# Layer 0 of a hybrid encoder in two halves, its projections first and in seven half products a pair

## The reference, cut to what matters

```python
def pool_mixer(h, w_in, w_group, scale, w_out):     # h = rms_norm(x, pool_norm)
    proj = h @ w_in                                  # (1024, 1024) @ (1024, 4096)
    u, gate = proj[..., :2048], proj[..., 2048:]
    ug = u.reshape(B, S, 4, 512)                     # four groups, windows 2, 4, 8, 16
    pooled = stack([centred_window_mean(ug[:, :, g], w) for g, w in enumerate((2, 4, 8, 16))])
    diff = pooled - ug
    mixed = einsum('bsgc,gcd->bsgd', diff, w_group).reshape(B, S, 2048) * scale
    return (mixed * silu(gate)) @ w_out              # (1024, 2048) @ (2048, 1024)
```

## Time and profile before

| | |
|---|---|
| median of 3 runs | 1842.08 us (1841.94 to 1842.33) |
| the profiled execution | 1842.04 us |
| its span | 1840.1 us |
| TensorE busy | 1823.5 us, 99% |
| VectorE busy | 872.9 us, 47% |
| ScalarE busy | 546.4 us, 30% |
| GpSimd busy | 154.0 us, 8% |

### The profile page before, as it was taken

One profiled execution on the slowest core, in us unless ns is written; L12 is line 12 of the kernel. 1 busy time (PEld: TensorE's weight loads), 2 busy tenths in 40 slices (PEclk: granted clock), 3 DMA queues, 4 the chain that ended last, 5 costly groups with the idle time before them and its releaser, 6 DMA issues.

```text
span 1840.1 us, 22883 instructions
## 1 busy us (share of the span) xinstructions
PE 1823.5 (99%) x8976; PEld 1538.2 (84%) x8976; DVE 872.9 (47%) x1728; ACT 546.4 (30%) x976; POOL 154.0 (8%) x236
## 2 busy tenths in 40 slices
PE   7999999999999999999999999999999999999999
PEld 7888888888888788888889888888888888888887
DVE  5544434633564543454156425523585415532575
ACT  4311211121221422343235424322421323422420
POOL 1000000000000410111011201110100101110100
PEclk9999999999999999999999999999999999999999
DMA  5211111111111421111111111111245111111234
GB/s 173 59 51 41 58 46 46 46 58 35 57 46 58 136 66 58 35 61 55 46 41 53 47 46 47 58 46 37 68 168 176 47 46 41 52 47 46 69 116 159
DMA packets 90506, 121.54 MB, mean 66 GB/s; under 512 B 14369, under 2 KB 52129, under 8 KB 90401
## 3 DMA queue, kind: packets, MB, share of 16 engines
q1 hardware_dynamic: 74304, 85.90, 15.3%
q10 hardware_dynamic: 16096, 34.19, 5.2%
HBM read 99.04 MB, written 21.04 MB: 65 GB/s over the span
## 4 chain that ended last, share of the span: by engine, by line
PE 97%; DVE 2%; DMA 0%; ACT 0%; issue 0%; POOL 0%; ACTq 0%; DVEq 0%; POOLq 0%
PE pair L617 28%; PE pair L619 28%; PE pair L618 28%; PE pair L841 4%; PE pair L819 4%; PE pair L809 2%; PE pair L828 2%; PE pair L630 0%; PE pair L797 0%; DMA xs<-in_x_dram 0%; DVE xs L895 0%; DVE hTl L911 0%; DVE bufS L919 0%; DVE bufU L919 0%; ACT squares L1257 0%
## 5 line engine op out<-in xcount | busy, mean ns | idle before, releaser
L617 PE MATMUL pair<-w,hTh 128*128 128x512 f32 x1280 | 515.3, 403 | 0.8 <-DVE xs L895 0.8
L619 PE MATMUL pair<-w,hTl 128*128 128x512 f32 x1280 | 500.7, 391 | 0.0
L618 PE MATMUL pair<-w,hTh 128*128 128x512 f32 x1280 | 499.4, 390 | 0.0
L619 PEld LDWEIGHTS pair<-w,hTl 128*128 128x128 f32 x1280 | 244.2, 191 | 50.7
L617 PEld LDWEIGHTS pair<-w,hTh 128*128 128x128 f32 x1280 | 244.6, 191 | 45.2 <-DVE xs L895 1.0
L618 PEld LDWEIGHTS pair<-w,hTh 128*128 128x128 f32 x1280 | 245.0, 191 | 43.9
L888 DVE TENSOR_TENSOR w<-raw,w 128x1024 fp32r<-128x1024 f32 x140 | 169.3, 1222 | 218.9 <-ACT w L1230 218.0
L617 PE MATMUL pair<-hTh,w 128*128 128x512 f32 (+1 forms) x560 | 209.0, 373 | 0.9 <-DVE hTl L911 0.9
L618 PE MATMUL pair<-hTl,w 128*128 128x512 f32 (+1 forms) x560 | 208.3, 372 | 0.0
L619 PE MATMUL pair<-hTh,w 128*128 128x512 f32 (+1 forms) x560 | 208.2, 372 | 0.0
L1230 ACT ACTIVATE w<-raw 128x1024 fp32r<-128x1024 f32 x144 | 149.8, 1052 | 141.7 <-PE pair L619 141.3
(11 more groups left out here) (119 smaller groups left out, 2200.1 us busy)
## 6 DMA issues: line engine op xcount, KB each, us to landing
raw<-in_att_w_in_dram SPq DMA_DIRECT2D x80, 512.0 KB, 3.7
raw<-in_pool_w_in_dram SPq DMA_DIRECT2D x32, 512.0 KB, 4.4
raw<-in_pool_w_out_dram SPq DMA_DIRECT2D x16, 512.0 KB, 3.4
u_spill<-ub ACTq DMA_DIRECT2D x32, 256.0 KB, 2.2
ub<-u_spill SPq DMA_DIRECT2D x32, 256.0 KB, 3.8
xb<-x_spill ACTq DMA_DIRECT2D x16, 512.0 KB, 4.4
xs<-in_x_dram ACTq DMA_DIRECT2D x8, 512.0 KB, 5.6
raw<-in_pool_w_group_dram SPq DMA_DIRECT2D x8, 512.0 KB, 3.5
```

What stands on the lines that cost most here:

```text
L617: nc.tensor.matmul(out, lh, rh, start=first, stop=False)
L618: nc.tensor.matmul(out, lh, rl, start=False, stop=False)
L619: return nc.tensor.matmul(out, ll, rh, start=False, stop=last)
```

## The change

Layer 0 gets two halves. In the first, all projections are made: six plain blocks (U(0,0..3), G(0,0), G(0,1)), then 13 couples of two feature blocks, U and G in turn. A couple is a product of a 256 x 1024 by a 1024 x 1024 matrix, taken as 2 x 2 blocks, in seven products (`couple`), each of 4 `kd` x 3 = 12 matmuls of 128x512. For that GpSimd adds high and low parts of the activations up again (`put_together`), VectorE makes four sums of their quarters (`turned_sums`) and ScalarE and VectorE split them once; for each couple GpSimd makes four sums of the weights' quarters (`weight_sums`), and ScalarE and VectorE split seven pieces of 512 (`split_product`) into a ring of ten half slots. The results stand in three banks X, Y and W; the three parts that two outputs share are copied out (`keep`) and added (`add_quarter`). The banks of odd and even couples differ. Raw buffers are freed in twos, after the low part of a couple's last piece.

The windows work in memory (`ubuf`), and diff and silu(gate) of every block are stored to DRAM: `diff_spill` and `gate_spill`, 16 blocks of 512 KB each. x is not kept: it is loaded again. In the second half come the M and O jobs of all groups, and diff and gate are loaded back into eight stage buffers in the room of the activations, over SyncE's queue. The calls of `split_hi`, `split_lo`, `diff_high`, `diff_low`, `z_first`, `z_high` and `z_low` there have the same operations and shapes as before, in a new order. The diff, cut to its core:

```diff
+    PLAIN = [("U", 0, 0), ("U", 0, 1), ("U", 0, 2), ("U", 0, 3), ("G", 0, 0), ("G", 0, 1)]
+    u_couples = [("U", g, h) for g in range(1, NG) for h in range(GB // 2)]
+    g_couples = [("G", 0, 1)] + [("G", g, h) for g in range(1, NG) for h in range(GB // 2)]
+    COUPLES = [k for both in zip(u_couples, g_couples) for k in both] + g_couples[len(u_couples):]
+    NCOUPLE, NPROD = len(COUPLES), 7
...
+        jobs = [("M", 0, 0)]
         for g in range(NG):
-            jobs.append(("U", g, 0))
-            if g:
-                jobs += [("O", g - 1, 1, tb) for tb in range(TB)]
-            jobs += [("U", g, c) for c in range(1, GB)]
-            jobs += [("G", g, 0), ("M", g, 0), ("G", g, 1), ("M", g, 1), ("G", g, 2)]
-            jobs += [("O", g, 0, tb) for tb in range(TB)]
-            jobs += [("M", g, 2), ("G", g, 3), ("M", g, 3)]
-        jobs += [("O", NG - 1, 1, tb) for tb in range(TB)]
-        pair_of = {j: n % 4 for n, j in enumerate(jobs)}
+            jobs += [("M", g, 1), ("M", g, 2)] + [("O", g, 0, tb) for tb in range(TB)] + [("M", g, 3)]
+            if g < NG - 1:
+                jobs.append(("M", g + 1, 0))
+            jobs += [("O", g, 1, tb) for tb in range(TB)]
...
+        def raw_released(u):
+            if NPLAIN <= u < LATER:
+                return w_lo, product((u - NPLAIN) // 2, NPROD - 1) + 1
+            return lo_ready(u)
...
-                    inverse_roots(layer, *range(TB))
+                    inverse_roots(layer, *range(5))
+                    for tb in range(TB):
+                        put_together(tb)
+                        if tb < 3:
+                            inverse_roots(layer, 5 + tb)
...
+            def put_together(tb):
+                pool.wait_ge(hlo_done, tb + 1)
+                tokens_ = slice(P * tb, P * tb + P)
+                nc.gpsimd.tensor_tensor(whole[:, :, tokens_], rowsh[:, :, tokens_].bitcast(F32),
+                                        rowsl[:, :, tokens_].bitcast(F32), ALU.add).then_inc(whole_set, 1)
+            def weight_sums(n):
+                for i in range(2):
+                    u = NPLAIN + 2 * n + i
+                    pool.wait_ge(raw_in[u % RAW], 16 * (u // RAW + 1))
+                if n:
+                    pool.wait_ge(w_lo, product(n - 1, 5) + 1)
+                else:
+                    pool.wait_ge(g_done, 2)
+                a11, a12, a21, a22 = (raw[:, 0, 0:512], raw[:, 0, 512:1024], raw[:, 1, 0:512], raw[:, 1, 512:1024])
+                nc.gpsimd.tensor_tensor(sums[0], a21, a22, ALU.add).then_inc(s_sum, 1)
+                pool.wait_ge(s_sum, 4 * n + 1)
+                nc.gpsimd.tensor_tensor(sums[1], sums[0], a11, ALU.subtract).then_inc(s_sum, 1)
+                nc.gpsimd.tensor_tensor(sums[2], a11, a21, ALU.subtract).then_inc(s_sum, 1)
+                pool.wait_ge(s_sum, 4 * n + 2)
+                nc.gpsimd.tensor_tensor(sums[3], a12, sums[1], ALU.subtract).then_inc(s_sum, 1)
...
+            def couple(n):
+                X, Y, W = couple_banks(n)
+                moving = [(X, lambda kd: (rowsh[:, kd, left], rowsl[:, kd, left])),
+                          (W, lambda kd: (rowsh[:, HB + kd, left], rowsl[:, HB + kd, left])),
+                          (X, lambda kd: (tone[:, HB + kd, left], tone[:, HB + kd, right])),
+                          (Y, lambda kd: (tone[:, kd, left], tone[:, kd, right])),
+                          (X, lambda kd: (ttwo[:, kd, left], ttwo[:, kd, right])),
+                          (Y, lambda kd: (rowsh[:, HB + kd, right], rowsl[:, HB + kd, right])),
+                          (X, lambda kd: (ttwo[:, HB + kd, left], ttwo[:, HB + kd, right]))]
+                for i, (out, rhs) in enumerate(moving):
+                    if i == 0:
...
+                    elif i == 2:
+                        pe.wait_ge(kept, 3 * n + 1)
+                        if n == 0:
+                            pe.wait_ge(t_lo, 4)
+                    elif i == 3:
+                        if n >= 2:
+                            pe.wait_ge(c_added, 3 * (n - 2) + 3)
+                    elif i == 4:
+                        pe.wait_ge(kept, 3 * n + 2)
+                    elif i == 5:
+                        pe.wait_ge(kept, 3 * n + 3)
+                    else:
+                        pe.wait_ge(c_added, 3 * n + 2)
+                    pe.wait_ge(w_lo, product(n, i) + 1)
+                    wh, wl = (product_view(n, i, lo).rearrange("p (k c) -> p k c", k=HB) for lo in (False, True))
+                    for kd in range(HB):
+                        rh, rl = rhs(kd)
+                        last = three(out, wh[:, kd, :], wl[:, kd, :], rh, rl, kd == 0 and i in (0, 1, 3),
+                                     kd == HB - 1, i not in (0, 1, 3))
+                    last.then_inc(prod_done, 1)
...
+            def turned_sums():
+                upper, lower = slice(0, KD // 2), slice(KD // 2, KD)
+                left, right = slice(0, T // 2), slice(T // 2, T)
+                b11, b12, b21, b22 = (whole[:, upper, left], whole[:, upper, right], whole[:, lower, left],
+                                      whole[:, lower, right])
+                dve.wait_ge(whole_set, TB)
+                nc.vector.tensor_tensor(b22, b22, b12, ALU.subtract).then_inc(t_sum, 1)
+                nc.vector.tensor_tensor(b12, b12, b11, ALU.subtract).then_inc(t_sum, 1)
+                dve.wait_ge(t_sum, 2)
+                nc.vector.tensor_tensor(b11, b22, b11, ALU.add).then_inc(t_sum, 1)
+                dve.wait_ge(t_sum, 3)
+                nc.vector.tensor_tensor(b21, b21, b11, ALU.subtract).then_inc(t_sum, 1)
+            def turned_low(i):
...
                 link(nc.vector.tensor_tensor(ends, ends, edge[:, g, :, :], ALU.mult))
-                mid = src[:, PAD:PAD + T]
-                nc.vector.scalar_tensor_tensor(out=mid, in0=mid, scalar=1.0 / w, in1=pair[pair_of[("U", g, c)]][:, :],
-                                               op0=ALU.mult, op1=ALU.subtract).then_inc(d_ready, 1)
-                split_lo(after(("U", g, c)))
+                nc.vector.scalar_tensor_tensor(out=u[:, PAD:PAD + T], in0=src[:, PAD:PAD + T], scalar=1.0 / w,
+                                               in1=u[:, PAD:PAD + T], op0=ALU.mult, op1=ALU.subtract).then_inc(d_ready, 1)
...
+            def add_quarter(n, i):
+                X, Y, W = couple_banks(n)
+                src, h, p, q, right = ((W, 0, 2, 0, 0), (X, 2, 5, 1, 1), (Y, 1, 6, 0, 1))[i]
+                kind, g, hh = COUPLES[n]
+                dve.wait_ge(prod_done, NPROD * n + p)
+                dve.wait_ge(kept, 3 * n + h + 1)
+                if i < 2:
+                    dve.wait_ge((d_out if kind == "U" else g_out)[q], 16 * (GB // 2 * g + hh))
+                dst = ubuf[:, q, PAD:PAD + T] if kind == "U" else gbuf[q][:, :]
+                nc.vector.tensor_tensor(dst[:, 512 * right:512 * right + 512], src, held[h], ALU.add).then_inc(c_added, 1)
+            def couple_windows(n):
+                kind, g, hh = COUPLES[n]
+                if kind == "U":
+                    dve.wait_ge(c_added, 3 * n + 3)
+                    window(g, 2 * hh)
+                    dve.wait_ge(c21_done, n + 1)
+                    window(g, 2 * hh + 1)
...
+            add_quarter(0, 0)
+            split_product(1, 0)
+            split_product(1, 1)
+            add_quarter(0, 1)
+            split_product(1, 2)
+            add_quarter(0, 2)
+            for i in range(3, NPROD):
+                split_product(1, i)
+            couple_windows(0)
+            for i in range(3):
+                split_product(2, i)
+            for n in range(1, NCOUPLE):
+                if n < NCOUPLE - 1:
+                    split_product(n + 1, 3)
+                    add_quarter(n, 0)
+                    for i in range(4, NPROD):
+                        split_product(n + 1, i)
+                    add_quarter(n, 1)
+                    add_quarter(n, 2)
+                    couple_windows(n)
+                    if n < NCOUPLE - 2:
+                        for i in range(3):
+                            split_product(n + 2, i)
+                    else:
+                        split_lo(LATER)
...
+                if 2 <= i < 6:
+                    act.wait_ge(s_sum, 4 * n + (2, 1, 3, 4)[i - 2])
+                p = NPROD * n + i
+                if p >= GRANULES - 2:
+                    act.wait_ge(*((prod_done, p - GRANULES + 1) if p >= GRANULES else (g_done, 2)))
+                elif p < 6:
+                    act.wait_ge(u_done, p // 2 + 2)
...
+            def keep(n, i):
+                X, Y, W = couple_banks(n)
+                act.wait_ge(prod_done, NPROD * n + (1, 3, 4)[i])
+                if n:
+                    act.wait_ge(c_added, 3 * (n - 1) + (1, 3, 2)[i])
+                else:
+                    act.wait_ge(g_done, 2)
+                nc.scalar.activation(held[i], (X, X, Y)[i], ACT.Copy).then_inc(kept, 1)
...
+            keep(0, 0)
+            for i in range(3, NPROD):
```

(79 more changed lines are left out.)

484 lines of the change are left out of this document (342 added, 142 removed).

## The result

| | before | after |
|---|---|---|
| median of 20 executions | 1841.98 us (1841.29 to 1842.85) | 1845.8 us (1842.95 to 1847.29) |
| the profiled execution | 1842.04 us | 1844.97 us |
| its span | 1840.1 us | 1842.4 us |

The ratio is 1.002, with a 95% interval of 1.0014 to 1.0026: slower by about as little as can be told from no change. The forecast was 1836.5 us and faster. The saving of 35.3 us came in full, and 37.6 us instead of 29.8 were given back: 35.3 and the 2.3 by which the profiled span is longer (by the medians, 3.8 us apart, it is 39.1).

What follows compares the result with a forecast made beforehand. TensorE's matmul count was taken as the bound while helpers stay hidden. Of 35.3 us saved, 29.8 would be returned, so 5.5 gained: 1842.0 to 1836.5 us, range 1814 to 1856.

Steps and rivals of the forecast that it cites:

- The saving of 35.3 us: Layer 0's thirteen couples: 84 matmuls instead of 96 each, 156 fewer at 0.226 us, saving 35.3 us.
- the pitch of 0.226 us: TensorE in layer 0: one 128x512 matmul starts 0.226 us after another, taken as the cost of each.
- rival 1: GpSimd's sums hardly hold VectorE up and the start stalls are short: 1812 to 1819 us, chance 0.2.
- rival 2: VectorE's chain of window steps keeps GpSimd's sums out until it ends: 1859 us, chance 0.13.
- start, until couple 0: Before the couples: GpSimd's put_together delays inverse roots and VectorE's scaling and low half, making TensorE wait: 3 us.
- couple 0, product 2: Plain projections cover the turned sums and four w=2 windows; if that fails, product 2 waits up to 3 us.
- couple 1's keep: ScalarE's copy stands behind splits of couple 2 that need late weights and sums: 6.1 us, paid once.
- behind windows of w=8 and 16: VectorE's addition for product 6 comes late after two windows slowed by GpSimd's sums: four stalls, 14.6 us.
- keeps behind late splits: Late splits delay loads and ScalarE's next keep; with gate stores, 0.8 after each of four G couples: 3.2 us.
- hand-overs and slower clock: Added for hand-overs and a slower clock behind the longer stalls: 2 us, a guess between 0 and 5.
- M and O jobs: Rest of layer 0 covered, except the last O weights' split after z at the end: 0.9 us.
- Rival 3: As forecast, but loads beside stores land 1 to 2 us later and the clock falls: 1842 to 1850 us, chance 0.2.

Runs made afterwards that it cites:

- no_sums: The changed kernel without GpSimd's four sums of each couple's weights, raw pieces split instead, so values differ from the reference; 1815.37 us, ratio 0.9857.
- keep_first: The changed kernel with ScalarE's copy of a couple's first product ahead of the next couple's three splits; 1837.97 us, ratio 0.9977.
- odd_window_later: The changed kernel with each U couple's second window moved on VectorE behind the next couple's splits and additions; 1827.8 us, ratio 0.9921.
- first_two: The changed kernel with keep_first and odd_window_later together, the start as changed; 1822.61 us, ratio 0.9893.
- held_4: The kernel before the change with TensorE held at six places of layer 0 by four small GpSimd operations each; 1891.94 us.
- held_2: The kernel before the change with TensorE held at six places of layer 0 by two small GpSimd operations each; 1871.58 us.
- held_9: The kernel before the change with TensorE held at six places of layer 0 by nine small GpSimd operations each; 1925.77 us.
- start_and_end: The changed kernel with keep_first, odd_window_later and roots_first, plus four further reorderings at the start, couple 1 and couple 12; 1816.05 us, ratio 0.9859.
- roots_first: The changed kernel with GpSimd making all eight inverse roots before adding up the activations; 1846.38 us, ratio 1.0023.
- all_three: The changed kernel with keep_first, odd_window_later and roots_first together; 1823.39 us, ratio 0.9895.
- held_1: The kernel before the change with TensorE held at six places of layer 0 by one small GpSimd operation each; 1851.6 us.

## Why the prediction was wrong

What was right: the pitch of 0.226 us and the 35.3 us; that VectorE's window steps and GpSimd's sums exclude each other and alternate, so that neither rival 1 nor rival 2 came; the places of the waits. The terms of what is given back, beside what they measured:

| term | forecast, us | measured, us |
|---|---|---|
| start, until couple 0 | 3 | 5.6 |
| couple 0, product 2 | 0 | 0.8 |
| couple 1's keep | 6.1 | 9.1 |
| behind windows of w=8 and 16 | 14.6 | 11.8 |
| keeps behind late splits | 3.2 | 2.5 |
| hand-overs and slower clock | 2 | 7.4 |
| M and O jobs | 0.9 | 0.4 |
| sum | 29.8 | 37.6 |

Couple 0 starts at 93.7 after, and by the rows of before would have started at 88.1; in the four other kernels with the same start (no_sums, keep_first, odd_window_later, first_two) it starts at 92.9 to 93.9, so this line is good to 1 us. From there to M(0,0), at 372.8, the 13 couples took 279.1 us. Undisturbed, three matmuls start every 0.68 us, a couple takes 84 / 3 x 0.68 = 19.04 and 13 take 247.5; of the 31.6 between, 24.2 are waits and 7.4 are not. Of these the clock behind the three long waits took 5.0 (1.50, 1.73 and 1.74). The other 2.4 go with the waits too: 9 x 0.16 in front of the brackets and 6 x 0.13 behind them are 2.2. They are no price of a couple, for in no_sums, with three short waits, the same 13 couples take 250.2 us and only 0.9 of that is neither pitch nor wait. The last term is what is left of the whole.

**The step that failed** is the term "2 us for hand-overs and for a slower clock behind the longer stalls", which measured 7.4, beyond the 5 that I gave as its upper end. The clock alone took 5 of it. The held kernels show how it is to be sized: 1.2 to 2 us for each wait of 3.3 us or more, and the forecast itself held three of those (6.1 and twice 4.9), so 4 to 6 us for the clock and not a part of 2; and 0.3 for every wait besides. Of the 7.8 us by which the sum was short, 5.4 are this term; with it alone put right the forecast is 35.2 given back of 35.3, no change. The other 2.4 are what is left of a start, a product 2 and a couple 1 that were too small by 6.4 together and window and keep waits, and the end, too large by 4.0; that so little is left of them is in part luck. Rival 3 had the clock's fall, and the measured time lies in its 1842 to 1850, but its other half, later loads, did not come: the weight loads of layer 0 list 5.0 us in the median, not over 6. Couple 1's wait was longer than forecast, with loads 0.3 us later, and the waits for additions and for the later keeps were shorter.

**Couple 1** was mis-sized too, 9.1 for 6.1. GpSimd's timeline there, and then ScalarE's:

```profile
122.97 1.98 POOL L775 TENSOR_TENSOR side<-raw 128x512 f32<-128x512 f32 x1 [7.96 <-DMA raw<-in_pool_w_in_dram]
125.03 2.33 POOL L777 TENSOR_TENSOR side<-side,raw 128x512 f32<-128x512 f32 x1
```

```profile
127.39 0.63 ACT L1605 ACTIVATE w0x<-side 128x512 fp32r<-128x512 f32 x1 [4.89 <-POOL side L777]
127.93 0.58 ACT L1713 ACTIVATE side<-pair 128x512 f32<-128x512 f32 x1
```

The weights land at 122.9, t = 29.2 for the 26.3 of the prediction, as the last split of couple 1 ended at t = 23.6 and not 21, and they landed 5.6 us behind it instead of 5.3. The two sums then take 4.3 us where 2.5 were given: they lie between w=4 windows, and I had charged the exclusion to VectorE alone. Over all 13 couples the second sum takes 1.89 us in the mean, alone it takes 1.29.

**The start.** The scaling behind each `put_together` lists 3.41 us for 1.28, as forecast (2.4 for the addition and 1.0 for itself), but four waits came of it, 0.73 and 0.76 for the scaled block (L1174) and twice 1.38 for the low half of the activations (L1166), 4.25 together. I had 0.9 (29.9 against 29.0), 0.3, 0.8 and 0.3 for the first kind and one of 0.9 for the second, 3.2 that I wrote as 3. The first kind came smaller, 1.5 for 2.3, the second larger, 2.8 for 0.9.

```profile
26.93 3.41 DVE L1174 SCALAR_TENSOR_TENSOR bufU<-xs,rstd,bufG 128x1024 f32<-128x1024 f32 x1 [0.72 <-POOL rstd L742]
```

The gain of 5.5 us was the difference of 35.3 and 29.8. An error of a quarter in the second turned its sign, and the terms that the trace before could not show (clock, start, couple 1) all came out too small. That trace has the exclusion, but the only long wait in it stands before TensorE's first instruction, so the clock's price had to come from a kernel like held_4. The range, 1814 to 1856, held the time; the half chance on faster was too much.

What is shown: the sums cause the waits in the couples (no_sums), behind the windows by the exclusion; the order decides whether they reach TensorE (odd_window_later, keep_first); and waits of 3.1 us and more cost clock (held_2 to held_9, start_and_end). What was only read from the trace after: couple 1's chain and the start's slack. Open: the 1.3 us of the start that are no wait, most of which the 0.29 beyond each of its four waits would make up by an estimate, and how much of couple 1's wait is exclusion.

## What to carry to other kernels

Work saved on the engine that is the bound is worth only what the helpers' queues let through: work out each wait that the new order brings, and where the rest is a small difference of two sums, call the sign open. In an in-order queue, put what the bound engine waits for (a copy that frees a bank, an addition that it accumulates onto) ahead of what waits for loads or for a third engine, and part long blocks of VectorE steps over two iterations; here that alone, with nothing computed differently, turned +3.8 us into -26.2. Look for a wait's successor before calling it mended: keep_first, roots_first and odd_window_later each let a new wait of 3.7 to 5.3 us in elsewhere.

## What the runs showed of the hardware

- VectorE with two inputs in SBUF and GpSimd exclude each other instruction by instruction, both ways: 1.24 to 2.2 us for VectorE's step, 1.29 to 2.3 for GpSimd's sum, and 0.18 to 1.15 for a step of 16 columns. 52 sums of 1.3 us, with the waiting for them, cost the kernel 30 us.
- TensorE's clock stays up behind waits of 1.0 to 2.5 us (2.48 in roots_first, 2.46 in all_three), and is 0.50 to 0.69 over the next 4 us behind each wait of 3.1 us or more in layer 0 of these kernels but one of 3.29 in held_2, where it stayed at 1.00 (the 9 us before the first matmul are not counted); the 4 us after that have 0.73 to 1.00. A wait of 12 us costs no more clock than one of 5.6.
- That 3.3 us would already lose clock was not what I expected of held_2: in the kernel as changed the waits lay either below 1.7 or above 4.2 us, and I had put the border higher.
- A wait at full clock costs 0.29 us more than the profile lists for it: 0.16 in front of it and 0.13 over the twelve matmuls behind (held_1, after, no_sums).
